# A decoder layer with 32 experts: gate and up weights in f16 halves, their bound by a matmul, the splits spread over an expert's two blocks

## The chip, the core and the metric

The kernel runs on one core of a Trainium2 chip. The metric is the device time of one execution in microseconds (us); lower is better. Engines are named as in the profile: PE (TensorE matmul) with PEld (its weight loads), DVE (VectorE), ACT (ScalarE), POOL (GpSimd) and SP (SyncE), which here only issues DMAs.

## What is computed

One hybrid decoder layer on 4096 tokens of width 1024, in float32 from outside. First a mixer (attention with a window of 128, and a gated short convolution), then a mixture of 32 experts: a router picks one group of four and two of its eight experts, so that there are 8192 pairs of a token and an expert. They are sorted by expert and worked off in blocks of 128 rows, each of one expert:

```
def expert_block(args):
    xb, e = args
    return (jax.nn.silu(xb @ w_g[e]) * (xb @ w_u[e])) @ w_d[e]

ybuf = lax.map(expert_block, (xbuf.reshape(n_blocks, MOE_BLK, D_MODEL), block_e))
y = ybuf.reshape(n_blocks * MOE_BLK, D_MODEL)[dest] * gate_s[:, None].astype(xt.dtype)
return jax.ops.segment_sum(y, tok_s, num_segments=n_tok)
```

`w_g` and `w_u` are 1024 x 512 for each expert and `w_d` is 512 x 1024, 2 MB each. The change touches this second half, the expert stage, alone.

## The kernel before, in words

**Precision.** A product of two float32 matrices is made of three matmuls: each operand is split into a high part (the value rounded to a narrower type) and a low part (what is left), and hi x hi, hi x lo and lo x hi are added up in PSUM. In the mixer (helper at L574) both parts are f16, and the operands are scaled by powers of two so that f16 can hold them. In the expert stage (helper `split_mm`, matmuls at L1676) both parts are fp32r, a float32 with a shortened mantissa, and nothing needs scaling. The profile shows an fp32r matmul as f32.

**One block of 128 rows on PE** (`tensor`, `block_`): 24 matmuls into psA (rows x gate weights), 4 transposes into psE of the previous block's product (`turn_act`, L1691), 24 matmuls into psB (rows x up weights), 8 transposes into psC and psD of the next block's rows (`transpose_rows`, L1684), and 24 matmuls into psF and psG (`down`), which are the down product of the block before. All matmuls have 512 columns. The first block of an expert follows the last of the expert before without a pause in the program.

**Splitting the weights.** SP loads an expert's three weights as float32 into `wi_all` (one buffer for each; `load_expert`, L172). ACT makes the high part (`split`, L1770, eight pieces of 512 columns, with a conversion to fp32r), DVE the low part as raw minus high (L1812, eight pieces). All of it is in the expert's first block: gate before that block's matmuls, up behind it, down at the end, when the down product of the expert before is done. There is one set of high and low parts for each weight, so the split of an expert's gate waits until the last psA of the expert before has been computed (`gate_ps`). SP issues the next load as soon as the split has read the buffer.

**The rest of a block.** On ACT and DVE, in their program order: `copy_y` (the down result of two blocks back, scaled by the row's gate, ACT L1777 and DVE L1819), `turn` (the transposed product in high and low part, L1789 and L1830), `silu` on ACT (L1783) and `product` on DVE (L1826), `turn_x` (the transposed rows in two parts, L1796 and L1836).

**The chain of the rows, on POOL** (`gpsimd`, `block_`): `shift` moves three short columns of indices along (two copies, L1617 and L1620); a DMA fetches the block's 128 slot entries (L1632); when they have landed and the transposes of the block before have read `xg`, an indirect DMA gathers the block's rows (`xg<-hn_rows`, L1600, 512 KB); when `copy_y` is done, POOL copies the row numbers (L1609) and an indirect DMA adds `y` to the output (L1612, 512 KB); then POOL waits until the gathered rows have landed and turns to the next block. PE's `transpose_rows` waits for those rows. Everything on POOL is in this one order.

**How many blocks.** `blocks_of` holds each expert's number of blocks, at least 1 (2 for expert 0). Every engine reads it and loops (`walk`).

**Passing from the mixer to the experts.** Each engine waits in `mixed` for the last table entries. Expert 0's three loads are issued before that. POOL then fetches the first slot entries and the first rows, and PE can begin.

## Time and profile before

| | us |
|---|---|
| median of 3 runs | 2751.67 (2751.11 to 2752.50) |
| the profiled execution, own time | 2750.93 |
| its span, first to last instruction | 2749.3 |
| PE busy in the span | 2643.6 (96%) |
| DVE busy | 1716.2 (62%) |
| ACT busy | 1391.3 (51%) |
| POOL busy | 798.8 (29%) |
| granted TensorE clock, mean of the span | 0.987 |

The profiled execution took 1.6 us more than its span, and lies 0.7 us under the median. A matmul's length in the profile reaches to its modelled end, and successive matmuls overlap; what one costs PE is the distance of the starts. In rows of the timeline with a count (x24), the piece's length reaches from the first start to the last end. In the chain of waits the pieces follow on each other, so that there a row's length is the time it takes of the span.

### The profile page before, as it was taken

Reading aid. Unit: us, or ns where it says so; the run is one execution under the profiler, and the core shown is the slowest. Engines: PE = TensorE matmul, PEld = TensorE weight load, DVE = VectorE, ACT = ScalarE, POOL = GpSimd, SP = SyncE. Lnnn points to the kernel's source line nnn. Section 1 sums busy time; section 2 is a strip of 40 time slices with the busy share of each in tenths; the row PEclk is TensorE's granted clock in tenths of the full one; section 3 lists DMA queues with packets and bytes.
Section 4 is the critical chain, followed back from the end, with each engine's and each line's share of the span. In section 5 each row is a group of like instructions: output and inputs, shape, how many; then the busy total and the mean of one; then the engine's idle time right before and its main releaser. Section 6 shows DMA issues by size and latency. Waiting matters only on the chain.

```text
span 2749.3 us, 49924 instructions
## 1 busy us (share of the span) xinstructions
PE 2643.6 (96%) x14252; PEld 1820.9 (66%) x14253; DVE 1716.2 (62%) x3920; ACT 1391.3 (51%) x3046; POOL 798.8 (29%) x825
## 2 busy tenths in 40 slices
PE   4999999999999999996699999999999999999997
PEld 2455555555555555553588888888888888888886
DVE  5677777777777777776454455545655444546633
ACT  7666555565555566553344445445545333435533
POOL 1122323232322222331232333323223323333232
PEclk9999999999999999998799999999999999999999
DMA  8376555556655555656556677667767665667763
GB/s 315 82 166 166 156 160 158 152 157 165 163 152 160 154 156 164 166 138 167 187 169 189 186 236 244 200 196 224 235 186 232 205 183 153 194 180 237 235 181 54
DMA packets 546395, 495.22 MB, mean 180 GB/s; under 512 B 411787, under 2 KB 411948, under 8 KB 545340
## 3 DMA queue, kind: packets, MB, share of 16 engines
q1 hardware_dynamic: 517516, 406.08, 49.2%
q0 software_dynamic: 28848, 88.77, 13.8%
q8 instruction: 14, 0.23, 0.0%
q14 instruction: 17, 0.14, 0.0%
HBM read 309.74 MB, written 87.88 MB: 145 GB/s over the span
## 4 chain that ended last, share of the span: by engine, by line
PE 89%; DVE 3%; DMA 3%; ACT 2%; issue 1%; SPq 1%; POOL 1%; POOLq 0%; DVEq 0%; ACTq 0%
PE psB L1676 15%; PE psA L1676 15%; PE psG L574 11%; PE psF L1676 7%; PE psG L1676 7%; PE psE L574 6%; PE psF L574 6%; PE psD L574 6%; PE psC L574 6%; PE psH L574 3%; PE psC L1684 1%; PE psD L1684 1%; PE psE L1691 1%; DMA xg<-hn_rows,slots 1%; DMA slots<-slot_table 1%
## 5 line engine op out<-in xcount | busy, mean ns | idle before, releaser
L574 PE MATMUL psG<-wi_all,both_xT 128*128 128x512 f16 x1536 | 345.2, 382 | 10.9 <-DMA both_xT<-x 10.9
L574 PEld LDWEIGHTS psG<-wi_all,both_xT 128*128 128x128 f16 x1536 | 148.7, 98 | 188.2 <-DMA both_xT<-x 11.1
L1600 POOL DMA_INDIRECT xg<-hn_rows,slots x80 | 99.2, 1240 | 544.0 <-DMA slots<-slot_table 389.4
L1676 PE MATMUL psB<-up_hi,gT_hi 128*128 128x512 f32 x632 | 254.4, 402 | 0.0
L1676 PE MATMUL psA<-gate_hi,gT_hi 128*128 128x512 f32 x632 | 247.3, 391 | 3.1 <-ACT gT_hi L1796 1.7
L1812 DVE TENSOR_TENSOR down_lo<-wi_all,down_hi 128x512 fp32r<-128x512 f32 x256 | 157.0, 686 | 147.1 <-ACT down_hi L1770 147.1
L1676 PE MATMUL psB<-up_hi,gT_lo 128*128 128x512 f32 x632 | 247.6, 392 | 0.0
L1676 PE MATMUL psA<-gate_hi,gT_lo 128*128 128x512 f32 x632 | 247.3, 391 | 0.0
L1676 PE MATMUL psA<-gate_lo,gT_hi 128*128 128x512 f32 x632 | 247.0, 391 | 0.0
L1676 PE MATMUL psB<-up_lo,gT_hi 128*128 128x512 f32 x632 | 246.4, 390 | 0.0
L1796 ACT ACTIVATE gT_hi<-psC 128x512 fp32r<-128x512 f32 x80 | 47.8, 597 | 384.8 <-PE psC L1684 384.8
L1826 DVE TENSOR_TENSOR act_rows<-psB,gated 128x512 f32<-128x512 f32 x79 | 54.6, 691 | 289.6 <-PE psB L1676 289.6
L1770 ACT ACTIVATE down_hi<-wi_all 128x512 fp32r<-128x512 f32 x256 | 137.0, 618 | 149.1 <-PE psG L1676 149.1
L819 ACT ACTIVATE prob<-prob,soft,s_stat 128x256 f32<-128x256 f32 x256 | 150.6, 589 | 94.2 <-DVE soft L1206 94.1
L1609 POOL COPY rows_of_y<-slots 128x1 int32<-128x1 int32 x80 | 129.3, 1616 | 236.9 <-DVE y L1819 236.2
L1812 DVE TENSOR_TENSOR gate_lo<-wi_all,gate_hi 128x512 fp32r<-128x512 f32 x256 | 157.0, 686 | 46.2 <-ACT gate_hi L1770 46.2
L574 PE MATMUL psE<-wo_all,both_mT 128*128 128x512 f16 x768 | 178.5, 383 | 5.9 <-DMA both_mT<-prob 5.9
L574 PE MATMUL psC<-wi_all,both_xT 128*128 128x512 f16 x792 | 178.6, 381 | 4.5 <-DVE wi_all L1186 4.5
L574 PE MATMUL psD<-wi_all,both_xT 128*128 128x512 f16 x792 | 178.2, 380 | 0.0
L574 PE MATMUL psF<-wo_all,both_mT 128*128 128x512 f16 x768 | 176.2, 379 | 0.0
L1770 ACT ACTIVATE gate_hi<-wi_all 128x512 fp32r<-128x512 f32 x256 | 137.0, 618 | 44.5 <-issue 44.5
L1812 DVE TENSOR_TENSOR up_lo<-wi_all,up_hi 128x512 fp32r<-128x512 f32 x256 | 156.7, 685 | 1.0 <-ACT up_hi L1770 1.0
(320 smaller groups left out, 5777.2 us busy)
## 6 DMA issues: line engine op xcount, KB each, us to landing
wi_all<-in_w_gate SPq DMA_DIRECT2D x32, 2048.0 KB, 9.5
wi_all<-in_w_up SPq DMA_DIRECT2D x32, 2048.0 KB, 12.9
wi_all<-in_w_down SPq DMA_DIRECT2D x32, 2048.0 KB, 11.7
xt<-in_x SPq DMA_DIRECT2D x32, 512.0 KB, 3.7
um<-u_rows SPq DMA_DIRECT2D x64, 256.0 KB, 2.7
out_rows<-h SPq DMA_DIRECT2D x32, 512.0 KB, 3.0
xres<-in_x SPq DMA_DIRECT2D x31, 512.0 KB, 4.1
hn_rows<-xres SPq DMA_DIRECT2D x31, 512.0 KB, 2.9
```

Source lines behind the costliest of these rows:

```text
L574: m = nc.tensor.matmul(ps, left[:, l, k, :], weights.half(r, k, n, width), start=(k == opens and j == 0), stop=(k == closes and j == 2))
L819: s.activation(prob[:, hd, :], prob[:, hd, :], ACT.Exp, bias=ntop[:, hd:hd + 1], scale=inv_s, accum_out=psum_[:, hd:hd + 1]).then_inc(p_sb ...
L1600: pool.indirect_dma_start(xg[:], None, hn_dram, bass.IndirectOffsetOnAxis(ap=slots[:, 0, 0:1], axis=0), bounds_check=SEQ + P - 1).then_inc ...
L1609: g.tensor_copy(rows_of_y[:], slots[:, 3, 0:1]).then_inc(named, 1)
L1676: m = nc.tensor.matmul(ps[:, :], l[:, k, :], r[:, r_k[n], :], start=(n == 0 and j == 0), stop=(n == len(l_k) - 1 and j == 2))
L1684: m = nc.tensor.transpose(ps[:, c * P:(c + 1) * P], xg[:, (4 * h + c) * P:(4 * h + c + 1) * P], ident)
L1691: m = nc.tensor.transpose(psE[:, c * P:(c + 1) * P], act_rows[:, c * P:(c + 1) * P], ident)
L1770: s.activation(hi[n][:, k, :], raw[n][:, k, :], ACT.Copy).then_inc(hi_s[n], 1)
L1796: s.activation(gT_hi[:, 4 * h:4 * h + 4, :].rearrange("p k c -> p (k c)"), ps[:, :], ACT.Copy).then_inc(xgT_hi, 1)
L1812: v.tensor_tensor(lo[n][:, k, :], raw[n][:, k, :], hi[n][:, k, :].bitcast(F32), ALU.subtract).then_inc(lo_s[n], 1)
L1826: v.tensor_tensor(act_rows[:], psB[:, :], gated[:], ALU.mult).then_inc(act_s, 1)
```

## The change

Gate and up are now in f16 parts. Since f16 has a small range, each of the two is multiplied by a power of two before the split, and the result is divided by it (`scale=inverse` in `silu`, and in `product`); the rows are scaled in `turn_x` by the known `hn_scale`. The power of two comes from a bound of the weights: ACT sums the absolute values of each partition's 4096 weights (`sum_up`, with a bf16 result that nobody reads), and the largest of the 128 sums is needed on every partition. For expert 0 POOL finds it (`partition_all_reduce`). For the others DVE masks the sums down to powers of two and spreads them on a diagonal (`spread_bound`), PE multiplies a matrix of ones with it (`every_bound`, 256 columns into psH), and DVE takes the maximum of the row and makes scale and inverse in five dependent steps (`scales`).

Gate and up have two raw buffers and two sets of parts (`p`), and are prepared an expert ahead: in the first block of expert e the gate of e+1 is split, in its second block the up of e+1; sums are taken another expert ahead. `down` stays in fp32r with one buffer, split in the first block. All splits are now two pieces of 2048 columns. Every expert has at least two blocks. PE waits for a whole weight, not for pieces of it.

The core of the diff; further hunks carry the scale into `silu`, `product` and `turn_x`, and unroll `walk` over pairs of experts:

```diff
-        step(v.tensor_scalar(blocks_of[:, counts], blocks_of[:, E:], 1, None, ALU.max))
-        step(v.tensor_scalar(blocks_of[:, 0:1], blocks_of[:, 0:1], 2, None, ALU.max))
+        step(v.tensor_scalar(blocks_of[:, counts], blocks_of[:, E:], 2, None, ALU.max))
...
-    hi = {n: sb(f"{n}_hi", [P, 8, 512], F32R) for n in raw}
-    lo = {n: sb(f"{n}_lo", [P, 8, 512], F32R) for n in raw}
+    hi = {n: [sb(f"{n}_hi_{p}", [P, 8, 512], F16) for p in range(2)] for n in SCALED}
+    lo = {n: [sb(f"{n}_lo_{p}", [P, 8, 512], F16) for p in range(2)] for n in SCALED}
+    hi["down"], lo["down"] = ([sb(f"down_{w}", [P, 8, 512], F32R)] * 2 for w in ("hi", "lo"))
...
+        def next_loads(e, p):
+            reload("gate", e + 1, 1 - p, 2)
+            reload("down", e, 0, 1)
+            reload("up", e + 1, 1 - p, 2)
+
+        sp.wait_ge(summed, 2)
+        for n in SCALED:
+            load_expert(sp, n, 1, 1)
         mixed(sp)
...
+        pool.wait_ge(summed, 2)
+        pool.partition_all_reduce(most(0), sums(0), P, RMAX).then_inc(most_s, 1)
         mixed(pool)
...
+        def every_bound(e):
+            pe.wait_ge(diagonal_s, 2 * e)
+            nc.tensor.matmul(every_row, ones[:, :], diagonal[:, :], start=True, stop=True).then_inc(every_s, 1)
...
+            if follow and (second if is_zero(e) else first):
+                every_bound(e + 1)
             if not static0:
                 turn_act(b)
...
+            s.activation(junk, raw[n][p].rearrange("p k n -> p (k n)"), ACT.Abs, accum_out=sums(p, n)).then_inc(summed, 1)
...
+            for c in range(CHUNKS):
+                s.activation(chunk(hi[n][p], c), chunk(raw[n][p], c), ACT.Copy, scale=power(p, n)).then_inc(hi_s[n], 1)
...
+            if is_zero(e) and first:
+                turn_x(b + 1)
+                sum_up("gate", 1, 1, 0, junk)
+                sum_up("up", 1, 1, 0, junk)
+                split_down(e, b)
...
+            v.tensor_scalar(most(p).bitcast(I32), sums(p).bitcast(I32), 0x7F800000, None, ALU.bitwise_and).then_inc(masked, 1)
+            dve.wait_ge(masked, e)
+            for c in range(2):
+                v.tensor_scalar(diagonal[:, c * P:(c + 1) * P], ident, most(p)[:, c:c + 1], None, ALU.mult).then_inc(diagonal_s, 1)
...
+                v.scalar_tensor_tensor(chunk(lo[n][p], c), chunk(raw[n][p], c), power(p, n), chunk(hi[n][p], c),
+                                       ALU.mult, ALU.subtract).then_inc(lo_s[n], 1)
```

How the order moves on the engines. On ACT, in an expert's first block before: gate split (L1770), `copy_y` (L1777), up split, `turn` (L1789), `silu` (L1783).

```order
343 L1768 ISA [waits gate_ps]
344 L1770 ACTIVATE gate_hi<-wi_all 128x512 [waits raw_in_gate]
345 L1770 ACTIVATE gate_hi<-wi_all 128x512 x7
346 L1774 ISA
347 L1775 REGISTER_ALU [waits y_ps]
348 L1776 ISA [waits shifted]
349 L1777 ACTIVATE y<-psF,slots 128x512 [waits added]
350 L1770 ACTIVATE up_hi<-wi_all 128x512 [waits raw_in_up,up_ps]
351 L1770 ACTIVATE up_hi<-wi_all 128x512 x7
352 L1788 REGISTER_ALU [waits aT_ps]
353 L1789 ACTIVATE aT_hi<-psE 128x512 [waits y_ps]
```

The same place now, from `silu` on: the gate split of the next expert (L1809), the rows (L1842), a sum (L1803, its junk result in `up_hi`), and the down split (L1816).

```order
360 L1829 ACTIVATE gated<-psA,own 128x512 [waits act_s,gate_ps]
361 L1807 ISA
362 L1809 ACTIVATE gate_hi<-wi_all,own 128x2048 [waits step_s]
363 L1809 ACTIVATE gate_hi<-wi_all,own 128x2048
364 L1841 ISA [waits up_ps]
365 L1842 ACTIVATE gT_hi<-psC,rt_stat 128x512 [waits xgT_ps]
366 L1841 REGISTER_ALU
367 L1842 ACTIVATE gT_hi<-psD,rt_stat 128x512 [waits xgT_ps]
368 L1800 ISA
369 L1802 REGISTER_ALU [waits raw_in_gate_1]
370 L1803 ACTIVATE up_hi,own<-wi_all 128x4096 [waits summed]
```

The up split has left this block for the second one, and no split stands ahead of `copy_y` any more. On DVE, at expert 0's first two blocks now: product, rows, the down split in two pieces (L1947), the mask (L1931) and the diagonal (L1935), and then the maximum over PE's answer (L1920).

```order
L1962 SCALAR_TENSOR_TENSOR act_rows<-psB,own,gated 128x512 [waits up_ps,silu_s]
L1973 SCALAR_TENSOR_TENSOR gT_lo<-psC,rt_stat,gT_hi 128x512 [waits xgT_hi]
L1973 SCALAR_TENSOR_TENSOR gT_lo<-psD,rt_stat,gT_hi 128x512 [waits xgT_hi]
L1947 TENSOR_TENSOR down_lo<-wi_all,down_hi 128x2048 [waits hi_s_down] x2
L1931 TENSOR_SCALAR own<-own 128x2 [waits summed]
L1935 TENSOR_SCALAR diagonal<-cst,own 128x128 [waits masked]
L1935 TENSOR_SCALAR diagonal<-cst,own 128x128
L1920 TENSOR_REDUCE own<-psH 128x2 [waits every_s]
```

PE's matmul for the bound waits for the diagonal, and so for all that stands above it here; PE does nothing else meanwhile, since it too is in program order.

## Rows read from the trace of the kernel before

**Rows 1.** The page: PE's busy time; costliest groups: ScalarE's silu, one a block.

```profile
PE 2643.6 (96%) x14252; PEld 1820.9 (66%) x14253; DVE 1716.2 (62%) x3920; ACT 1391.3 (51%) x3046; POOL 798.8 (29%) x825
...
L1783 ACT ACTIVATE gated<-psA 128x512 f32<-128x512 f32 x79 | 46.8, 593 | 4.0 <-PE psA L1676 4.0
```

**Rows 2.** Chain that ended last, two late blocks: start us, us, what.

```profile
2692.97 5.44 PE psA L1676 x24
2698.42 0.44 PE psE L1691 x4
2698.86 5.49 PE psB L1676 x24
...
2710.68 5.44 PE psA L1676 x24
```

**Rows 3.** Timeline of PE in the mixer: start us, us, instructions.

```profile
409.53 5.34 PE L574 MATMUL psG<-wi_all,both_xT 128*128 128x512 f16 x24
414.71 2.78 PE L574 MATMUL psH<-wi_all,both_xT 128*128 128x256 f16 x24
```

**Rows 4.** Timeline of ACT: gate splits of an expert of two blocks and its successor.

```profile
1856.32 4.28 ACT L1770 ACTIVATE gate_hi<-wi_all 128x512 fp32r<-128x512 f32 x8 [1.13 <-issue]
...
1891.78 4.28 ACT L1770 ACTIVATE gate_hi<-wi_all 128x512 fp32r<-128x512 f32 x8 [1.18 <-issue]
```

**Rows 5.** Groups by line: ACT and DVE work on other widths.

```profile
L791 ACT ACTIVATE wi_all<-wi_all 128x2304 bf16<-128x2304 f32 x8 | 17.0, 2122 | 4.7 <-DMA wi_all<-in_w_in 4.7
L779 ACT ACTIVATE x<-xt,stat 128x1024 f16<-128x1024 f32 x33 | 37.9, 1148 | 1.1
L1276 DVE SCALAR_TENSOR_TENSOR x<-xt,stat,x 128x1024 f16<-128x1024 f32 x33 | 42.2, 1280 | 8.5 <-ACT x L779 8.5
L1327 DVE SCALAR_TENSOR_TENSOR q<-qsq,q 128x512 f16<-128x512 f32 x32 | 22.2, 693 | 5.9 <-ACT q L891 5.4
```

**Rows 6.** Timeline around an expert's second block (psA from 1877.5): DVE, SP, POOL, PE.

```profile
1883.28 0.75 DVE L1819 TENSOR_SCALAR y<-psG,slots 128x512 f32<-128x512 f32 x1
1883.51 0.37 SPq L172 DMA_DIRECT2D wi_all<-in_w_down  x1
1885.49 1.65 POOL L1612 DMA_INDIRECT out_rows<-y,rows_of_y  x1 [0.96 <-DMA xg<-hn_rows,slots]
1888.53 0.59 POOL L1632 DMA_DIRECT2D slots<-slot_table  x1 [0.85 <-POOL slots L1620]
1896.84 1.89 POOL L1600 DMA_INDIRECT xg<-hn_rows,slots  x1 [7.71 <-DMA slots<-slot_table]
1898.36 4.90 DVE L1812 TENSOR_TENSOR up_lo<-wi_all,up_hi 128x512 fp32r<-128x512 f32 x8
1898.76 4.55 POOL L1609 COPY rows_of_y<-slots 128x1 int32<-128x1 int32 x1
...
1906.58 0.60 PE L1684 MATMUL psC<-cst,xg 128*128 128x128 f32 x4
```

**Rows 7.** By tile, from issue to landing: the 80 gathers (xg); then y's.

```profile
DMA to landing us min/median/max: 4.2/4.5/9.8
...
DMA to landing us min/median/max: 5.9/9.9/11.1
```

**Rows 8.** Timeline at the start of the experts: POOL and SP.

```profile
1318.77 0.62 POOL L1632 DMA_DIRECT2D slots<-slot_table  x1 [5.41 <-DVE y L1844]
1321.69 1.21 POOL L1600 DMA_INDIRECT xg<-hn_rows,slots  x1 [2.30 <-DMA slots<-slot_table]
1322.79 0.38 SPq L172 DMA_DIRECT2D wi_all<-in_w_gate  x1
...
1333.65 1.09 POOL L1600 DMA_INDIRECT xg<-hn_rows,slots  x1 [5.39 <-DMA slots<-slot_table]
```

**Rows 9.** Timeline of PE: after an idle time, and just behind.

```profile
1275.64 5.04 PE L574 MATMUL psE<-wo_all,both_mT 128*128 128x512 f16 x12 [5.86 <-DMA both_mT<-prob]
1280.52 2.75 PE L574 MATMUL psF<-wo_all,both_mT 128*128 128x512 f16 x12
```

More of the change, by code:

```diff
@@ new lines, in is_zero, with split_up, reload @@
+    def is_zero(e):
+        return isinstance(e, int) and e == 0
+    def sync(sp):
+        def split_up(n, e):
+            sp.wait_ge(hi_s[n], CHUNKS * (e + 1))
+            sp.wait_ge(lo_s[n], CHUNKS * (e + 1))
+        def reload(n, e, p, ahead):
+            split_up(n, e)
+            load_expert(sp, n, e + ahead, p)
+        def next_loads(e, p):
[5 more added lines that the diff above has]
+            load_expert(sp, n, 1, 1)
+        mixed(sp)
+        reload("gate", 0, 0, 2)
+        reload("up", 0, 0, 2)
+        with sp.Fori(0, (E - 4) // 2) as pair:
+            next_loads(pair * 2, 0)
+            next_loads(pair * 2 + 1, 1)
+        next_loads(E - 4, 0)
+        reload("down", E - 3, 0, 1)
+        reload("down", E - 2, 0, 1)
@@ L1782, in silu @@
                 act.wait_ge(act_s, b)
-            s.activation(gated[:], psA[:, :], ACT.Silu).then_inc(silu_s, 1)
+            s.activation(gated[:], psA[:, :], ACT.Silu, scale=inverse(p, "gate")).then_inc(silu_s, 1)
         def turn(b):
@@ L1796, in turn_x, with block_ @@
                 s.activation(gT_hi[:, 4 * h:4 * h + 4, :].rearrange("p k c -> p (k c)"), ps[:, :],
-                             ACT.Copy).then_inc(xgT_hi, 1)
+                             ACT.Copy, scale=hn_scale).then_inc(xgT_hi, 1)
+        def block_(e, i, b, p, r, follow):
+            known = isinstance(b, int)
+            first, second = isinstance(i, int) and i == 0, isinstance(i, int) and i == 1
+            junk = hi["up"][1 - p][:].rearrange("p k n -> p (k n)").bitcast(BF16)
+            if not (known and b < 2):
+                copy_y(b)
+            if not (known and b == 0):
+                turn(b)
+            silu(b, p)
+            if is_zero(e) and first:
[3 more added lines that the diff above has]
+                split_down(e, b)
+            elif is_zero(e) and second:
+                split("gate", 1, 1)
+                turn_x(b + 1)
+                sum_up("gate", 2, 0, 1, junk)
+                sum_up("up", 2, 0, 1, junk)
+                act.wait_ge(summed, 6)
+                split("up", 1, 1)
+            elif first:
+                if follow:
+                    split("gate", e + 1, 1 - p)
+                turn_x(b + 1)
+                if follow > 1:
+                    sum_up("gate", e + 2, p, r + 1, junk)
+                split_down(e, b)
+            elif second:
+                if follow > 1:
+                    sum_up("up", e + 2, p, r + 1, junk)
+                turn_x(b + 1)
+                if follow > 1:
+                    act.wait_ge(summed, 2 * (e + 3))
+                if follow:
+                    split("up", e + 1, 1 - p)
+            else:
+                turn_x(b + 1)
@@ L1799, in scalar @@
         s.preload_act_table_set("silu_and_others")
+        for c, n in enumerate(SCALED):
+            sum_up(n, 0, 0, 0, wi_flat[:, 12288 + c * 2048:12288 + (c + 1) * 2048].bitcast(BF16))
         mixed(act)
         act.sem_inc(y_act, 3)
-        halves(act, split, copy_y, silu, turn, turn_x)
+        split("gate", 0, 0)
+        turn_x(0)
+        split("up", 0, 0)
+        total = walk(act, block_)
+        copy_y(total)
+        turn(total)
+        copy_y(total + 1)
     def vector(dve):
@@ L1835, in turn_x, with block_ @@
                 dve.wait_ge(xgT_hi, 2 * b + h + 1)
-                v.tensor_tensor(gT_lo[:, 4 * h:4 * h + 4, :].rearrange("p k c -> p (k c)"), ps[:, :],
-                                gT_hi[:, 4 * h:4 * h + 4, :].rearrange("p k c -> p (k c)").bitcast(F32),
-                                ALU.subtract).then_inc(xgT_lo, 1)
+                hold(dve, held)
+                v.scalar_tensor_tensor(gT_lo[:, 4 * h:4 * h + 4, :].rearrange("p k c -> p (k c)"), ps[:, :], hn_scale,
+                                       gT_hi[:, 4 * h:4 * h + 4, :].rearrange("p k c -> p (k c)"),
+                                       ALU.mult, ALU.subtract).then_inc(xgT_lo, 1)
+        def block_(e, i, b, p, r, follow):
+            known = isinstance(b, int)
+            first, second = isinstance(i, int) and i == 0, isinstance(i, int) and i == 1
+            if not (known and b < 2):
+                copy_y(b)
+            if follow and (second if is_zero(e) else first):
+                scales(e + 1, 1 - p)
+            if not (known and b == 0):
+                turn(b)
+            if follow and (second if is_zero(e) else first):
+                split("gate", e + 1, 1 - p)
+            product(b, p)
+            turn_x(b + 1)
+            if first:
+                split_down(e)
+            if is_zero(e) and first:
+                spread_bound(1, 1)
+            if second and follow:
+                split("up", e + 1, 1 - p)
+            if second and follow > 1:
+                spread_bound(e + 2, p)
         v.memset(slots[:], 0).then_inc(cleared, 1)
@@ L1842, in vector @@
         v.tensor_copy(slots[:, :, 0], cst[:, C_JUNK:C_JUNK + 1].to_broadcast([P, 4])).then_inc(cleared, 1)
+        scales(0, 0)
         mixed(dve)
+        v.memset(ones[:], 1.0)
         v.memset(y[:], 0.0).then_inc(cleared, 1)
         dve.sem_inc(y_dve, 3)
-        halves(dve, split, copy_y, product, turn, turn_x)
+        split("gate", 0, 0)
+        turn_x(0)
+        split("up", 0, 0)
+        total = walk(dve, block_)
+        copy_y(total)
+        turn(total)
+        copy_y(total + 1)
     return dict(sync=sync, tensor=tensor, scalar=scalar, gpsimd=gpsimd, vector=vector)
```

220 lines of the change are left out of this document (124 added, 96 removed).

## The prediction

> **What bounds the kernel now.** I read the page first: PE is busy for 96% of the span [rows 1], so only what shortens or interrupts PE counts. Then the chain of waits, for one late block [rows 2]: from one psA (2692.97) to the next (2710.68) are 17.71 us, in which every piece follows on the last with no gap. There are 79 blocks, with one silu each [rows 1]; 78 x 17.71 = 1381 of the 2749 us. Inside, 24 matmuls of psA take 5.44 us, 0.227 us each, and the 24 of psB 5.49. The mixer has the other price: 24 f16 matmuls of the same 512 columns run from 409.53 to 414.71, 5.18 us or 0.216 each [rows 3]. ACT and DVE are half idle over the span, but the splits come in bursts, and POOL's chain of the rows has little room in it: these decide whether PE gets its gain.
>
> **The change, part by part.**
>
> *Cheaper matmuls.* In each block 48 of 72 matmuls become f16. Gain (5.44 - 5.18) x 2 = 0.52 us a block, x 79 = 41 us. The first psB matmul stands behind short transposes, so that its weight load shows: psB takes 0.05 more than psA [rows 2]. An f16 load is quicker; I take 0.07 us a block, 6 us (bounds 0 and 12). Together -47.
>
> *More blocks?* Not here. The 32 gate splits in the trace of ACT never start closer than 35 us, which is two blocks, and 1856.32 to 1891.78 [rows 4] is such a pair. The new minimum of two adds none.
>
> *The bound on PE.* 31 matmuls of 256 columns. In the mixer 24 such columns-of-256 go from 414.71 to 417.33, 0.109 each. With a weight load that may show behind it 0.14, x 31 = +4 (bounds 3 and 7).
>
> *ACT and DVE in the steady state.* Prices: ACT takes 1148 ns for 1024 columns to f16 with a scale, and 2122 for 2304 to bf16 [rows 5]. Between them 2048 columns come to 2.0 us, and a sum over 4096, at the same 0.8 to 0.9 ns a column, to 3.8 with its read-out. DVE takes 693 and 1280 ns [rows 5]: 2.4 to 2.5 us for 2048. Now walk through an expert of two blocks, F being the start of its first psA. PE: psA ends at 5.2, bound 5.3, psB ends 11.0, transposes 11.9, down 17.3. DVE: scales in five steps 5.5 to 6.9. ACT: `turn` and `silu` to 7.0, gate split to 11.0, rows 11.5 to 12.6, gate sum to 16.4, down split from 17.4 to 21.2. DVE: `turn` to 7.6, low gate 9.1 to 13.9, product 14.6, rows 15.9. The next psA needs those rows at 17.3: room 1.4. Second block, T = 17.3: DVE ends the low down at T+6.8 and `copy_y` at T+7.4; the down product needs them at T+11.7. ACT: up sum T+6.9 to T+10.7, rows to T+12.5, up split to T+16.4. DVE: low up to T+19.3, 2.2 into the next expert; PE needs it at T+22.7. The diagonal follows 1 us later, needed at T+22.3. So nothing stops PE: 0, and the cover is these rooms of 1.4 to 4 us. One expert's splits and sums are 19 us of ACT in 34.4, beside 6 of small work.
>
> *POOL's chain.* `copy_y` of the second block ends at T+7.4. Before, from its end (1884.03) to the issue of the slot entries (1888.53) are 4.5 us, and 7.7 + 0.6 later (1896.84) the gather starts [rows 6]. So slot entries at T+11.9, gather at T+20. Its rows are needed at the next block's transposes, T+17.1+11.0 = T+28.1: the gather may take 8. The median is 4.5, the longest 9.8 [rows 7]. The gather of [rows 6] is one of the long: issued at 1896.84, it feeds transposes that start at 1906.58, just in time. Behind it POOL's copy stands for 4.55 us, until DVE's run of low parts ends (1903.3). I read both as POOL being held up by DVE. In the changed order DVE's low up ends at T+19.3, ahead of this gather, and the next copy waits for a `copy_y` with no split near. What is new is the up load, issued at T+19.4, just ahead of the gather. y's adds to the output, the size of a gather, show what a load does: 5.9 at best, 9.9 in the median [rows 7], and the one of [rows 6] goes out 2 us behind a load. With two thirds of that surcharge I take 7.5 for the gather: the rows land at T+27.5, and in some of the 28 experts that have an up load there PE waits a little. +4 (bounds 0 and 28 x 1.7 = 48, for 9.8).
>
> The Trainium skill, "GPSIMD Engine Reference", section Specifications, has the SBUF interfaces of POOL shared with DVE, in contention when a DVE instruction has two SBUF inputs. By that rule each low part of 2.4 us can hold up a POOL copy falling into it; the 4.55 us of [rows 6] agree. If the rule caught the copies of every second block, PE would lose what the second rival below has; by the walk it doesn't.
>
> *The start, gather.* Before, the first slot entries are issued at 1318.77 and the gather starts at 1321.69 [rows 8], with no load in flight. Now POOL waits for two sums on ACT (7.7 us together, begun when the mixer lets go of ACT some 10 us ahead of those slot entries, so to about 1317) and the reduction, of which I assume 0.5: slot entries at about 1319.5. And SP issues two loads, 4 MB, at 1317. The next gather shows what that does: POOL waited 5.39 us for its slot entries, issued some 5 us after the load of 1322.79, against 2.30 for the first [rows 8]. With two loads ahead I take 8 us to landing. First rows at about 1334.5 instead of 1326.4: +8 (bounds +3 and +14).
>
> The skill speaks for less. "DMA: Bandwidth & Descriptors", section Queues, rings and completion order, says that each DMA engine takes turns between queues packet by packet, so that a small transfer would wait for one packet of a load and not for the load. By that rule the start would lose some 3 us, and the sum would be 5 lower. The 5.39 of [rows 8] lies nearer to a whole load, so I keep 8.
>
> *The start, bound.* The stall this change adds in plain sight. S is the psA start of expert 0's second block. ACT ends the rows at S-1, takes two sums (7.7) and the two pieces of the down split (3.8); DVE's second low piece ends at S+13.2, the diagonal at S+14.1. PE stands at S+5.2, waiting for that diagonal, with the transposes and psB queued behind it. +8.9. After 5.86 us without work PE took 5.04 us for 12 matmuls that take 2.75 right after [rows 9]: it had come back at the lower of its clocks, 1.2 GHz. The same here: +2.3. Together +11.
>
> *Sum.* 2750.9 - 47 + 4 + 4 + 8 + 11 = 2731, for an execution 0.7 us under the median of the runs, which I leave uncorrected. Tail and mixer stay.
>
> **The rivals.**
>
> 1. *The rows come late in every expert* (slower). Place: PE's transposes in an expert's first block, when their gather starts just behind an up load. Price: as it takes 9.8 instead of 7.5, T+29.8 against T+28.1, 1.7 x 28 = 48, less the 4 counted: 2731 + 44 = 2775. It decides from about 8.6 us on, where the loss is 0.5 an expert and more; above 9.2 the kernel is slower. For it: the longest gathers, and the adds' median. Against: the long gathers seem to have another cause, DVE, which the new order takes away. 0.13.
>
> 2. *DVE's splits run longer* (no change). A low part could cost as much as the slowest work of its kind in the trace, 1.66 ns a column, 3.4 us. Then the low gate ends at F+15.9, the rows at F+17.9, and PE stands 0.6 in 31 experts, 19 us: 2750. Against: that happens beside POOL's long products in the mixer, which the expert stage hasn't. With halves of rival 1, 0.13.
>
> 3. *The start is hidden.* The slot entries pass the loads, and the diagonal is ready earlier than I count: 2731 - 16 = 2715. Against: both are in program order. 0.08.
>
> 4. *f16 gives nothing here*, because something else than the operand's type sets 0.227: 2731 + 41 = 2772. The mixer's even 5.18 speaks against. 0.02.
>
> **How the numbers follow.** My forecast, 0.64: 2731, with 2722 to 2743 from its own bounds (gather 4 at the start, small waits 0 to 10). The range has to leave out no more than 0.2: downwards it takes in most of rival 3, upwards rival 2 and the lighter half of rival 1, 2718 to 2758. A change of 0.2%, 5.5 us, is what a measurement of this kernel can tell from none. Faster by more: forecast and rival 3, 0.72. Within: rival 2, 0.13. Slower: rivals 1 and 4, 0.15.
>
> **What the profile after would show.** A late block of 17.1 us in the chain, psA and psB at 5.18 to 5.2 (else rival 4). PE idle once for about 9 us at L1761, in the second block of the stage, released by DVE's diagonal, with the granted clock at half behind it. The first gather's rows at about 1334. PE's idle time for `xg` under 10 us in total; if it is 30 or more, with gathers of 9 us, rival 1. If PE waits for DVE's gT_lo in first blocks, and the low parts take over 3 us, rival 2. By the sum the expert stage, from its first psA to its last psG, is 28 us shorter than before; if it is not 15 to 40 shorter, the sum is wrong.

## The result, and the profile after

The changed kernel takes 2793.5 us (median of 4 runs, 2790.9 to 2800.0), the one before 2751.6 beside it: ratio 1.0155, 95% interval 1.0136 to 1.0175. It is slower by 42 us, where 2731 was predicted and 2758 was the end of the range. The profiled execution took 2790.9, its span 2789.3.

The page, engine times, chain by engine, and the group of POOL's gathers (total us, mean ns, idle before):

```profile
PE 2625.4 (94%) x14283; PEld 1494.0 (54%) x14284; DVE 1759.5 (63%) x3598; ACT 1603.3 (57%) x2598; POOL 738.2 (26%) x826
...
PE 72%; DMA 13%; DVE 5%; ACT 3%; issue 3%; POOL 1%; SPq 1%; POOLq 1%; ACTq 0%; DVEq 0%
...
L1651 POOL DMA_INDIRECT xg<-hn_rows,slots x80 | 129.3, 1616 | 446.9 <-DMA slots<-slot_table 216.2
```

PE is busy 18 us less than in [rows 1] (38 less in the run without low parts, e2_reduce, where it stalls only at the start: matmuls at the lower clock count as busy for longer), and its share is lower all the same: it waits. The groups by line say for what (PE's transposes of the rows and the bound's matmul) and give the prices of the new pieces:

```profile
L1733 PE MATMUL psC<-cst,xg 128*128 128x128 f32 x320 | 52.7, 291 | 67.0 <-DMA xg<-hn_rows,slots 66.5
...
L1761 PE MATMUL psH<-diagonal,ones 128*128 128x256 bf16 x31 | 8.6, 276 | 8.1 <-DVE diagonal L1935 8.1
...
L1803 ACT ACTIVATE up_hi<-wi_all 128x4096 bf16<-128x4096 f32 x62 | 224.2, 3617 | 0.2
L1941 DVE SCALAR_TENSOR_TENSOR up_lo<-wi_all,own,up_hi 128x2048 f16<-128x2048 f32 x64 | 147.7, 2349 | 42.1 <-ACT up_hi L1809 42.1
L1809 ACT ACTIVATE gate_hi<-wi_all,own 128x2048 f16<-128x2048 f32 x64 | 124.7, 1995 | 15.0 <-DVE own L1924 15.0
```

Of the 66.5 us for rows, 23.6 are the one wait at the start; 42.8 are ten waits of 4.0 to 4.4 us and one of 0.2 in the steady part.

The sharpest measure is the distance from one silu (ScalarE, once a block) to the next, 78 of them. Before they sum to 1379.2 us, 17.68 each. After, 66 of them are 16.2 to 17.7, mean 17.21; **two at the start are 23.2 and 20.8; and ten more are 23.0 to 24.3.** Against 17.1 each the ten cost 63.4 us and the two 9.8. So 1379.2 - 38.2 + 63.4 + 9.8 = 1414.2, and the first psA begins 6.8 us later (1336.63 against 1329.82): +41.8. The way from the first psA to the first silu is 1.4 us shorter than before, the tail 0.4: 40.0, which is the difference of the two spans.

Nine of the ten fall into the second block after an expert of two blocks, behind three gathers in a row of 8 us or more. The tenth, the earliest, falls into the second block after expert 0, where the rows come after slots entries of 6.0 and 6.5 us and a gather of 10.0. Not every expert of two blocks brings one: of sixteen (the last expert left out) seven bring none, and each of these directly follows one that did, whose stall has moved the next gathers off the loads. The chain of waits through one of the ten (start us, us, what):

```profile
1911.10 5.20 PE psA L1725 x24
1916.30 0.44 PE psE L1740 x4
1916.73 5.18 PE psB L1725 x24
...
1927.95 1.72 DVE up_lo L1941
1929.67 9.29 DMA xg<-hn_rows,slots
...
1940.77 1.57 POOL slots_old L1668
...
1943.47 6.11 DMA slots<-slot_table
...
1950.57 9.98 DMA xg<-hn_rows,slots
1960.55 0.04 issue
1960.60 1.11 PE psC L1733 x4
1961.71 0.85 PE psD L1733 x4
1962.57 3.49 PE psF L1725 x12
1966.05 2.72 PE psG L1725 x12
```

psA and psB cost 5.20 and 5.18, as forecast. Then two gathers of 9.3 and 10.0 us, with a slots entry of 6.1 and a copy of 1.6 between them, are one serial chain on POOL, from 1929.67 to 1960.55. From the start of one gather to the start of the next are 20.9 us, where a block leaves 17.1. PE waits 4.2 us for the second, and comes back at the lower clock. Stretches behind it (us, busy, then granted clock, DMA share, GB/s):

```profile
1958.00:1960.00 2.00, 0.00 (x0) 0.00 (x0) 0.00 (x0) 0.00 (x0) 0.00 (x0) 1.00 0.94 301
1960.00:1962.00 2.00, 1.40 (x7) 1.40 (x8) 0.00 (x0) 0.25 (x1) 0.37 (x2) 0.65 1.07 281
1962.00:1964.00 2.00, 2.00 (x7) 1.68 (x6) 1.32 (x2) 1.83 (x3) 0.59 (x1) 0.50 0.79 171
1964.00:1966.00 2.00, 2.00 (x10) 1.60 (x9) 0.86 (x2) 2.00 (x2) 0.76 (x1) 0.99 0.00 0
```

A granted clock of 0.50 is 1.2 GHz; the transposes and psF take 5.45 us there, and some 3.65 in a block without a stall.

What meets the gathers: SP's queue in the same stretch, all loads of 2 MB.

```profile
1908.07 0.37 SPq L172 DMA_DIRECT2D wi_all<-in_w_gate  x1
...
1930.44 0.37 SPq L172 DMA_DIRECT2D wi_all<-in_w_up  x1
1942.53 0.37 SPq L172 DMA_DIRECT2D wi_all<-in_w_gate  x1
1952.27 0.37 SPq L172 DMA_DIRECT2D wi_all<-in_w_down  x1
```

The gathers start at 1906.55, 1929.67 and 1950.57. **Each of three gathers in a row has a load issued 1.5, 0.8 and 1.7 us behind it**, and they land after 9.9, 9.3 and 10.0 us. Of 80 gathers 47 take 8 us or more; before, 9 did.

### The profile page after: what moved, and what is told of

It is laid out like the page before. It is cut to its first block, busy times and chain, and to the rows that moved or that the text cites. A ratio compares the mean times of both kernels' runs of the same rounds, so it can differ in the third digit from the quotient of the medians.

```text
span 2789.3 us, 48388 instructions
## 1 busy us (share of the span) xinstructions
PE 2625.4 (94%) x14283; PEld 1494.0 (54%) x14284; DVE 1759.5 (63%) x3598; ACT 1603.3 (57%) x2598; POOL 738.2 (26%) x826
## 4 chain that ended last, share of the span: by engine, by line
PE 72%; DMA 13%; DVE 5%; ACT 3%; issue 3%; POOL 1%; SPq 1%; POOLq 1%; ACTq 0%; DVEq 0%
PE psG L575 11%; PE psB L1725 9%; PE psA L1725 9%; DMA xg<-hn_rows,slots 8%; PE psE L575 6%; PE psF L575 6%; PE psD L575 6%; PE psC L575 6%; PE psF L1725 5%; PE psG L1725 5%; DMA slots<-slot_table 4%; PE psH L575 3%; DVE up_lo L1941 1%; PE psC L1733 1%; PE psD L1733 1%
## 5 line engine op out<-in xcount | busy, mean ns | idle before, releaser
L575 PE MATMUL psG<-wi_all,both_xT 128*128 128x512 f16 x1536 | 345.2, 381 | 11.2 <-DMA both_xT<-x 11.2
L1725 PE MATMUL psA<-gate_hi,gT_hi 128*128 128x512 f16 x632 | 241.0, 381 | 3.7 <-issue 2.0
L1725 PE MATMUL psB<-up_hi,gT_hi 128*128 128x512 f16 x632 | 240.5, 381 | 0.0
L1725 PE MATMUL psB<-up_lo,gT_hi 128*128 128x512 f16 x632 | 240.3, 380 | 0.0
L1725 PE MATMUL psB<-up_hi,gT_lo 128*128 128x512 f16 x632 | 240.3, 380 | 0.0
L1725 PE MATMUL psA<-gate_lo,gT_hi 128*128 128x512 f16 x632 | 240.0, 380 | 0.0
L1725 PE MATMUL psA<-gate_hi,gT_lo 128*128 128x512 f16 x632 | 240.0, 380 | 0.0
L1803 ACT ACTIVATE up_hi<-wi_all 128x4096 bf16<-128x4096 f32 x62 | 224.2, 3617 | 0.2
L1947 DVE TENSOR_TENSOR down_lo<-wi_all,down_hi 128x2048 fp32r<-128x2048 f32 x64 | 143.8, 2288 | 109.3 <-ACT down_hi L1816 109.3
L1941 DVE SCALAR_TENSOR_TENSOR up_lo<-wi_all,own,up_hi 128x2048 f16<-128x2048 f32 x64 | 147.7, 2349 | 42.1 <-ACT up_hi L1809 42.1
L1941 DVE SCALAR_TENSOR_TENSOR gate_lo<-wi_all,own,gate_hi 128x2048 f16<-128x2048 f32 x64 | 147.7, 2349 | 42.1 <-ACT gate_hi L1809 42.1
L1842 ACT ACTIVATE gT_hi<-psC,rt_stat 128x512 f16<-128x512 f32 x80 | 55.0, 687 | 171.5 <-PE psC L1733 170.6
```

The source lines that it names most:

```text
L575: m = nc.tensor.matmul(ps, left[:, l, k, :], weights.half(r, k, n, width), start=(k == opens and j == 0), stop=(k == closes and j == 2))
L1725: m = nc.tensor.matmul(ps[:, :], l[:, k, :], r[:, r_k[n], :], start=(n == 0 and j == 0), stop=(n == len(l_k) - 1 and j == 2))
L1803: s.activation(junk, raw[n][p].rearrange("p k n -> p (k n)"), ACT.Abs, accum_out=sums(p, n)).then_inc(summed, 1)
L1842: s.activation(gT_hi[:, 4 * h:4 * h + 4, :].rearrange("p k c -> p (k c)"), ps[:, :], ACT.Copy, scale=hn_scale).then_inc(xgT_hi, 1)
L1941: v.scalar_tensor_tensor(chunk(lo[n][p], c), chunk(raw[n][p], c), power(p, n), chunk(hi[n][p], c), ALU.mult, ALU.subtract).then_inc(lo_s[n ...
L1947: v.tensor_tensor(chunk(lo["down"][0], c), chunk(raw["down"][0], c), chunk(hi["down"][0], c).bitcast(F32), ALU.subtract).then_inc(lo_s["do ...
```

## The experiments

Theory T1: the load in flight makes the gathers long, and PE late. Rival T2: DVE's long two-input low parts hold POOL, whatever the loads do. A joint theory, that it takes both, came out of the first runs. "Sum" is that of the 78 silu distances; "held" counts gathers whose issue on POOL lasts 1.5 us or more instead of 1.06. Sum and counts are those of one profiled execution.

| kernel | us | sum | gathers over 8 us | held | distances over 20 us |
|---|---|---|---|---|---|
| before | 2751.6 | 1379.2 | 9 | 12 | 0 |
| after | 2793.5 | 1414.2 | 47 | 37 | 12 |
| e1_gated | 2739.6 | 1357.6 | 1 | 29 | 3 |
| e2_reduce | 2733.8 | 1351.1 | 9 | 2 | 2 |
| e3_start | 2790.1 | 1416.8 | 49 | 40 | 12 |
| e4_later | 2791.4 | 1408.7 | 49 | 37 | 10 |
| e5_f16 | 2719.8 | 1345.1 | 13 | 16 | 0 |
| e6_all | 2728.0 | 1354.9 | 1 | 29 | 1 |
| e7_spread | 2793.4 | 1414.2 | 45 | 39 | 12 |
| e8_best | 2726.4 | 1353.4 | 1 | 28 | 2 |
| e9_f16_held | 2723.5 | 1352.7 | 2 | 11 | 2 |
| e10_pieces | 2730.1 | 1354.4 | 31 | 31 | 3 |
| e11_ahead | 2736.1 | 1350.9 | 30 | 23 | 2 |
| e12_f16_ahead | 2715.8 | 1342.6 | 16 | 4 | 1 |

Runs are medians of 4; before, beside them, 2752.3 to 2755.0.

### e1_gated: loads held back

```diff
-            reload("gate", e + 1, 1 - p, 2)
+            reload("gate", e + 1, 1 - p, 2, first_in)
             reload("down", e, 0, 1)
-            reload("up", e + 1, 1 - p, 2)
+            reload("up", e + 1, 1 - p, 2, second_in)
```

SP waits besides until the rows of expert e+1's first, or second, block have landed, which POOL counts in two new semaphores.

> The changed kernel, but SP issues an expert's gate load only when the rows of the next expert's first block have landed, and its up load when those of the next expert's second block have; the down load comes behind the gate load in the same queue. Theory T1 (the late rows in ten experts come from the gather of rows, 512 KB, being in flight together with a 2 MB expert load that is issued within about 2 us of it: 8.4 to 10.4 us instead of 4.5, twice in a row in experts of two blocks): the gathers take 4.4 to 5.5 us, the ten silu gaps of 23 to 24.3 us outside the first expert go back to 17.1 to 17.6, the time falls by about 62 us to some 2730. Rival T2 (DVE's long two-input low parts hold POOL's gather descriptors and copies, whatever the loads do): gathers stay at 8 us or more, ten long gaps stay, time 2785 to 2795. If the loads now arrive too late for ACT's sums, new stalls show on ACT and the time is between.

Measured: 2739.6 us, ratio to before 0.9939 (0.9922 to 0.9956). DVE's work is untouched and 29 gathers are still held at issue, but they now take 4.9 to 6.5 us (one, at the start, 10.2), and no long distance is left behind the fourth. POOL's gather in the place that corresponds to 1950.57:

```profile
1930.80 2.22 POOL L1654 DMA_INDIRECT xg<-hn_rows,slots  x1 [4.46 <-DMA slots<-slot_table]
1935.26 0.19 POOL L1663 COPY rows_of_y<-slots 128x1 int32<-128x1 int32 x1 [2.24 <-DVE y L1959]
```

T2 alone falls. DVE's low part of down starts at 1929.80 in two pieces of 2.29: the gather is held to the end of the first, 1932.09, and 0.94 us beyond. The time missed 2730 by 10: the first four distances (24.5, 20.9, 16.6, 21.7) are 6.4 us more than the changed kernel's, and in this execution the mixer ended 6 us later.

### e2_reduce: DVE's low parts with one input

```diff
+                if not isinstance(e, int):
+                    v.tensor_reduce(scrap[:, c:c + 1], chunk(raw[n][p], c), AX, ALU.max).then_inc(lo_s[n], 1)
+                    continue
```

> The changed kernel, but from expert 2 on DVE's low parts of gate and up (two-input, 2.35 us each) are left out: in their place stands a maximum over the same 2048 raw elements into a scratch column, with the same semaphores, so the low matmuls read the low parts of the first experts. T1 (gather and load collide): gathers with a load issued within 2 us still take 8.4 to 10 us, though their issue on POOL falls to 1.06 us; at least seven of the ten long gaps stay; time 2765 to 2793. T2 (DVE holds POOL): gathers back to 4.5 us, no long gap, time about 2730.

The kernel leaves these low parts out; the maximum in their place keeps DVE busy for 2.28 us instead of 2.35.

Measured: 2733.8, 0.9923 (0.9907 to 0.9940). T1 alone falls too. The loads come as before, but the gathers' issue is down to 1.06 us, and a load issued 1.4 us behind them hurts no more: they take 4.2 to 4.8 us, where the changed kernel has 9.2 to 10.0 with a load 1.5 us behind. With the load 0.1 to 0.8 us behind they still take 4.8 to 8.8. So it is both: **the load has to fall into the gather's issue, and DVE's low part stretches that issue until it does.** Gathers of the 14 profiles, by when the next load is issued (count, median, lowest to highest, us):

| load behind the gather's start by | issue under 1.5 us | issue 1.5 us or more |
|---|---|---|
| no load from 9 ahead to 5 behind | 372: 4.4 (4.2 to 7.5) | 100: 5.3 (4.7 to 6.5) |
| 0 to 0.9 | 99: 8.9 (4.8 to 10.1) | 32: 9.2 (8.4 to 9.7) |
| 0.9 to 1.6 | 28: 4.5 (4.2 to 7.1) | 116: 9.7 (8.3 to 10.2) |
| 1.6 to 1.9 | 9: 4.8 (4.6 to 7.7) | 19: 10.0 (9.8 to 10.5) |

The DMA packets in the traces say what decides: whose packets start first. POOL's transfers are in queue q0, SP's loads in q1. First the changed kernel from the start of the gather at 1906.55 to 1911.95, then the kernel without low parts from the start of such a gather, at 1881.79 (issue 1.06 us, load 1.4 behind), until it has landed, at 1886.25 (packets, MB, share of the 16 engines):

```profile
q1 hardware_dynamic: 343, 0.70, 46.9%
...
q0 software_dynamic: 144, 0.52, 39.8%
q1 hardware_dynamic: 78, 0.16, 15.5%
```

In the first, 343 packets of the load have started before the first of the gather, which comes at 1911.97; in the second the gather's 144 go ahead. A gather's first packet comes 0.70 us after the end of its issue when nothing is in the way, a load's most often 1.0 to 1.2 us after its own issue. **Of 282 gathers with a load issued up to 2.6 us behind their start, no other load issued in the 11 us before and no add of `y` in flight (all profiles but e9_f16_held, the first three gathers left out), 222 had it issued 0.37 us or more before the end of their own issue, and took 5.8 to 11.2 us; the 60 others had it 0.24 before that end at the earliest, and took 4.2 to 5.3.** The load overtakes, and a held issue gives it the time to.

The two are bound to meet: SP issues a load when DVE's low part ends, and a gather that falls into a piece of it is held to that piece's end. In the changed kernel, a gate's low part and the gather:

```profile
1903.21 4.61 DVE L1941 SCALAR_TENSOR_TENSOR gate_lo<-wi_all,own,gate_hi 128x2048 f16<-128x2048 f32 x2 [1.34 <-ACT gate_hi L1809]
...
1906.55 2.21 POOL L1651 DMA_INDIRECT xg<-hn_rows,slots  x1 [6.69 <-PE psD L1733]
```

DVE ends at 1907.82, the load follows at 1908.07, and POOL's issue ends at 1908.76. The Trainium skill, "SBUF — State Buffer", section "SBUF: two separate sides", has such starvation for transfers whose descriptors GpSimd writes while DVE holds the port pair they share; the 2.21 against 1.06 us agree. The Trainium skill, "DMA: Bandwidth & Descriptors", section "Queues, rings and completion order", has the DMA engines take turns between queues; by that rule alone a load 0.5 us behind would be no worse than one 1.4 behind, and the rows differ, 8.9 against 4.5. Between 1909.09 and 1911.97 no turn of the gather is seen; whether its packets were ready by then the trace doesn't tell.

### e3_start: late first loads

```diff
         sp.wait_ge(summed, 2)
+        mixed(sp)
+        sp.wait_ge(rows_in, 16)
         for n in SCALED:
             load_expert(sp, n, 1, 1)
-        mixed(sp)
```

> The changed kernel, but the early loads of expert 1's gate and up are issued only when the first rows have landed. The first slots entry takes 2 to 3 us instead of 5.1, the first gather 4.5 instead of 5.6; the first psA begins 3 to 6 us sooner against the mixer's end. By T1 the rest of the run is unchanged or one long gap more or less: 2784 to 2790. If the start was not held by these loads (T2 has no loads in it): within 2 us of 2791.

Measured: 2790.1, 1.0130 (1.0113 to 1.0147). From the mixer's last psH to the first psA are 23.1 us instead of 27.5 (before 21.7), so the loads did cost 4.4. The first distance grew to 24.4 and gave 1.2 of it back.

### e4_later: the bound of expert 1 later

PE's `every_bound(1)` goes behind `transpose_rows`, DVE's `scales` and both gate splits behind `turn_x`, in expert 0's second block only.

> The changed kernel, but in expert 0's second block the bound's matmul stands behind PE's transposes of the next rows, and the scales and the gate split behind the turn of x on DVE and ACT. If the 8.1 us wait of PE for the diagonals, with the half clock behind it, cost the 9.8 us that the two first silu gaps are over 17.1 each: the first two gaps together fall from 44.0 to 34 to 37 us and the time falls by 7 to 10 us, to 2781 to 2784. If that block waits for its rows anyway (T1: the gathers of that stretch are long too), under 3 us.

Measured: 2791.4, 1.0133 (1.0111 to 1.0155): no gain. The wait moved on; PE's long waits now (its idle time in brackets):

```profile
1369.23 0.28 PE L1761 MATMUL psH<-diagonal,ones 128*128 128x256 bf16 x1 [1.59 <-DVE diagonal L1937]
...
1393.74 0.77 PE L1725 MATMUL psF<-down_hi,aT_hi 128*128 128x512 f32 x1 [6.20 <-DVE aT_lo L1968]
```

DVE, with scales and the gate split now at the end of that block, comes 6.2 us late to the next block's `turn`.

### e5_f16: f16 halves alone

```diff
-    hi = {n: sb(f"{n}_hi", [P, 8, 512], F32R) for n in raw}
+    hi = {n: sb(f"{n}_hi", [P, 8, 512], F32R if n == "down" else F16) for n in raw}
```

The same for `lo` and for `gT_hi`, `gT_lo`, in the kernel before; no scaling.

> The kernel before, with one thing changed: the halves of gate, up and of the turned rows are f16 instead of f32r, without scaling; sums, bounds, the spread splits and the earlier loads are all left out. Step of the prediction: psA and psB of 24 matmuls take 5.2 us instead of 5.45 each, so 41 to 47 us less: 2704 to 2710, if the loads and gathers stay where they were. T1: a shorter block shifts the loads against the gathers a little, but DVE and ACT keep the short pieces of 512, and the second block's gather keeps its room; at most one or two long gaps. T2: same. If the f16 gain itself is missing (the rival that f16 gives nothing): 2750.

Measured: 2719.8, 0.9880 (0.9863 to 0.9896). A late block of its chain:

```profile
2611.46 5.20 PE psA L1676 x24
2616.66 0.44 PE psE L1691 x4
2617.10 5.18 PE psB L1676 x24
...
2628.65 5.20 PE psA L1676 x24
```

17.19 us instead of 17.71 [rows 2], x 78 = 41. It gains 32.5; some 7 us go into distances of 17.4 to 18.1. Thirteen gathers take 8 us or more, each with a gate load issued between 0.4 us ahead of its start and 1.3 behind. They are what the 2704 to 2710 expected left out.

### e6_all: e1_gated, e3_start and e4_later together

> The changed kernel with the three edits together: loads held until rows have landed, first loads after the first rows, the bound of expert 1 behind the transposes. T1 and the prediction's terms for start and bound: 2791 less 62, less 3 to 6, less 7 to 10, so 2712 to 2720. T2: above 2765.

Measured: 2728.0, 0.9910 (0.9893 to 0.9926), outside the 2712 to 2720 expected; of the 59 us by which the sum falls, to 1354.9, the held loads alone give 57. In the first blocks PE waits 6.24 us for `aT_lo`, as in the run with the bound later.

### e7_spread: the diagonals before down's low parts

`spread_bound(1, 1)` stands ahead of `split_down(0)` on DVE.

> The changed kernel, but in expert 0's first block DVE makes the diagonals of expert 1 before the low parts of down, not behind them. If PE's wait of 8.1 us for the diagonal comes from DVE's order (4.5 us of low parts and ACT's down halves ahead of it), that wait falls to 0 to 3 us, the first silu gap from 23.2 to 17 to 19 us, and no later gap grows by as much: time 2782 to 2786. If ACT's second sum (the up weights landing late) is what sets it, the wait stays over 5 us and the time within 3 us of 2791.

Measured: 2793.4, 1.0144 (1.0127 to 1.0161), where 2782 to 2786 was expected. PE's wait for the diagonal is gone, the first distance falls only to 21.1, the second grows to 21.5, and the time is the same. In its place:

```profile
1351.96 0.66 PE L1733 MATMUL psC<-cst,xg 128*128 128x128 f32 x4 [2.54 <-DMA xg<-hn_rows,slots]
1355.06 0.58 PE L1725 MATMUL psA<-gate_hi,gT_hi 128*128 128x512 f16 x1 [2.01 <-issue]
```

The second rows came late, and some twelve matmuls behind them ran at the lower clock.

### e8_best: e1_gated, e3_start and e7_spread together

> The changed kernel with three edits: loads held until rows have landed, expert 1's first loads after the first rows, and the diagonals before down's low parts. Expected from the runs with the loads held and with the late first loads: 2740 less 4 for the start, less 6 to 9 for the two first blocks: 2724 to 2730; if the late first loads set the second sum now, 2730 to 2736.

Measured: 2726.4, 0.9903 (0.9886 to 0.9919). The first four distances together are 7 to 15 us over 17.1 each in every one of these versions, whatever is moved there.

### e9_f16_held: f16 alone, gate load held

```diff
                 sp.wait_ge(lo_s[n], 8 * e)
+                if n == "gate":
+                    sp.wait_ge(second_in, 8 * e)
```

POOL counts `second_in` up when the rows of an expert's second block have landed. This kernel and e12_f16_ahead also ask for two blocks of every expert, which each has anyway.

> The kernel before with f16 halves alone (as in the run of that kind, 2720), and besides its gate load held until the rows of the same expert's second block have landed. There 13 gathers still took 8 us or more, each with a gate load issued 0 to 0.8 us behind it while DVE made up's low parts, and the silu gaps over 17.2 us summed to about 7 us. By the joint theory (load right behind a gather, and DVE's low part stretching the gather's issue) no gather is over 7 us and the time is 2712 to 2716. If those gaps come from POOL's copies under DVE's work instead, the gathers shorten but the gaps stay: 2718 to 2722.

Measured: 2723.5, 0.9890 (0.9863 to 0.9916): a miss. The holding SP queue lets gate and up loads go together, half a microsecond apart, and the slots entry then stands behind 4 MB. POOL there:

```profile
1865.33 0.60 POOL L1636 DMA_DIRECT2D slots<-slot_table  x1 [0.77 <-POOL slots L1624]
1874.38 1.12 POOL L1604 DMA_INDIRECT xg<-hn_rows,slots  x1 [8.45 <-DMA slots<-slot_table]
```

8.45 us for 1 KB, and its gather took 7.1.

### e10_pieces: eight short pieces instead of two long

`CHUNKS = 8` instead of 2.

> The changed kernel with all halves made in eight pieces of 512 elements instead of two of 2048. Joint theory (what counts is that DVE is at a two-input low part while POOL issues the gather, and that the load follows on its end): pieces back to back hold POOL as two long ones do, the gather's issue still takes over 1.5 us in some 30 blocks, eight or more long gaps stay, time 2785 to 2800. Rival T3 (only one long instruction holds POOL, short ones let it in between): issue 1.06 to 1.3 us, gathers of 4.5 to 5 us with the load 1.4 us behind, at most three long gaps, 2735 to 2750.

Measured: 2730.1, 0.9911 (0.9894 to 0.9927): 63 us won by one constant. The joint theory's number fell, and T3's range is missed by 5 us on the better side, though only half of its reason holds. The gather that meets the gate's low part goes free:

```profile
1870.82 5.39 DVE L1941 SCALAR_TENSOR_TENSOR gate_lo<-wi_all,own,gate_hi 128x512 f16<-128x512 f32 x8
...
1875.41 1.07 POOL L1651 DMA_INDIRECT xg<-hn_rows,slots  x1 [4.83 <-PE psD L1733]
```

0.80 us of DVE's run are left at its start, and it is issued in 1.07 us; in the changed kernel, with one long piece, a gather with 0.8 us left took 1.79. What counts is the piece that runs when the gather starts, here with 0.14 us left. Where more than 0.12 us of a piece are left, the issue ends 0.94 us after the end of that piece in 322 of 322 cases with long pieces and in 131 of 169 with short ones (all profiles, the first three gathers left out). The load comes 1.0 us behind, and the gather lands in 4.5 us instead of 9.9. With down's pieces too a gather got in early (3.6 us of the run left, issue 1.53; with long pieces 2.34). But the one that meets the up's low part is held through one piece more, the last, to 1898.80 and 0.94 us beyond, and takes 9.6:

```profile
1893.42 5.38 DVE L1941 SCALAR_TENSOR_TENSOR up_lo<-wi_all,own,up_hi 128x512 f16<-128x512 f32 x8
...
1897.69 2.06 POOL L1651 DMA_INDIRECT xg<-hn_rows,slots  x1 [6.42 <-DMA slots<-slot_table]
```

31 gathers still take 8 us or more. That the time is down nonetheless is the point: the first of the three bad gathers in a row takes 5 us less, so the third starts earlier beside down's low part, its load comes 3.8 us behind it instead of 1.7, and it takes 4.9. Only the one in the middle stays long, and the ten stalls are one (22.5). In that one the second and the third are long, 8.7 and 10.2, so two in a row can be enough.

### e11_ahead: the slots entry one block ahead

```diff
-            pool.dma_start(slots[:, 0, :], table[bass.ds(e * CAP + i * P, P), :]).then_inc(slots_in, 16)
+            if fixed and not (known and b == 0):
+                pool.wait_ge(slots_in, 16 * (b + 1))
...
+                g.tensor_copy(slots[:, 0, :], ahead[:, i, :]).then_inc(placed, 1)
...
             gather()
+            if fixed and i == 0:
+                pool.dma_start(ahead[:, 1, :], table[bass.ds(e * CAP + P, P), :]).then_inc(slots_in, 16)
...
```

Behind the gather of a second block POOL fetches the entry of the next expert's first block in the same way.

> The changed kernel, loads and splits untouched, but POOL fetches the slots entry of an expert's first and second block one block ahead (a copy of 0.2 us takes the place of the fetch of 2 to 7 us between the landing of one block's rows and the next gather). If a gather of 9 to 10 us only hurts because that fetch stands in series with it on POOL (entry 6.2, gather 10, copies 1.6 to 4 us: more than the 17.1 us of a block), then gathers of 8 us or more stay, as many as in the changed kernel or more, but the ten long silu gaps vanish: 2726 to 2733. If the long gather alone makes the rows late, the gaps stay: 2780 to 2793.

Measured: 2736.1, 0.9938 (0.9921 to 0.9954), 3 us over the 2726 to 2733 expected. 30 gathers still take 8 us or more, and not one costs anything: behind the third no distance is over 17.4. A bad one, and who releases it now:

```profile
1914.62 0.19 POOL L1689 COPY slots<-ahead 128x2 int32<-128x2 int32 x1 [0.33 <-POOL slots L1673]
1918.02 2.22 POOL L1653 DMA_INDIRECT xg<-hn_rows,slots  x1 [3.22 <-PE psD L1749]
```

The gather goes out as soon as PE has read the last rows. The sum equals that of the run without low parts; the median is 2 us over it, and in this execution a load 1.8 us behind the very first gather made it 10.5 us.

### e12_f16_ahead: the same on e5_f16

> The kernel before with f16 halves alone (2720) and the slots entry fetched one block ahead in the same way. Its silu gaps of 17.4 to 18.1 us, 7 us in sum over 17.2, come from gathers that are issued late behind the entry's fetch and then meet the gate load. Expected: no gap over 17.3 us outside the first blocks, 2711 to 2715. If the gaps come from POOL's copies that wait through DVE's low parts, they stay: 2718 to 2722.

Measured: 2715.8 (2709.0 to 2719.3), 0.9856 (0.9839 to 0.9872), the fastest kernel of the study; with the f16 halves alone it was 0.9880 (0.9863 to 0.9896), so the intervals overlap and that it beats that one isn't shown. It misses the 2711 to 2715 expected by 1 us, and one distance of 22.5 is left in its profile, at a third block, whose entry isn't fetched ahead.

## Why the prediction was wrong

**Failed: POOL's chain.** The prediction walked one gather, that of the up load, and priced it at 7.5 us, +4. The chain cost 63. Three things were wrong with it.

- *Its price and its cause.* "I read both as POOL being held up by DVE" and "In the changed order DVE's low up ends at T+19.3, ahead of this gather". The low part ends at 1930.3, T+19.2, as walked, but the gather starts at 1929.67, 0.6 us before that and not at T+20. It took 9.3 us. The hold alone makes 4.7 to 6.5.
- *The ones not walked.* Gate and down loads follow on DVE's low parts just as the up load does, and the gathers they met, one ahead of the up's and one behind it, took 9.9 and 10.0 us.
- *The stall's place.* The 9.3 us gather landed at T+28, just in time, as the walk would have had it. The next one was late: entry 6.1, copy 1.6, gather 10.0 in series. The added slots entry of [rows 6] was in the walk once, not as a term that recurs.

The trace of before had the other half of the cause. Its gather of 1896.84 [rows 6] took 9.6 us with a gate load issued 1.2 us behind it, a row that the reading left out:

```profile
1898.01 0.37 SPq L172 DMA_DIRECT2D wi_all<-in_w_gate  x1
```

All nine of its gathers of 8 us or more have a gate load 0.5 to 1.4 us behind their start; the six others whose issue took 1.5 us or more landed in 4.7 to 4.9, with the next load 2.1 or more behind.

Rival 1, "the rows come late in every expert", had the right resource, and 0.13 of the chance. It had the wrong count, 28 for ten: experts of three blocks recover, with a gather that meets no load, and of the experts of two blocks in a row every other one is spared. And its price lacked the clock: ten stalls at 6.3 us, of which some 4 are the wait (4.2 in the chain above) and 2 the lower clock behind it. Measured +63 where the sum had +4.

**Right, by the prediction's own steps.** psA and psB at 5.20 and 5.18. Blocks without a stall are 17.21 in the mean, the bound's matmul included, against 17.68. That makes -38 over the 78 distances, where -47 and +4, so -43, were taken. The further 6 us for psB's first weight load are not there: a late block of f16 alone is 17.19, against the 17.12 of the working. No more blocks. The sum 3.8 us and the halves 2.0 on ACT, as taken; DVE's 2.35 a little under it, so rival 2 is out. Start: +6.8 for +8, of which 1.0 is that the mixer ended later in this execution (slots entry 5.1, where 8 was taken; gather 5.6). Bound: an idle 8.1 us for 8.9, 9.8 with the clock for 11. But moving that wait away gave nothing in two runs, since DVE's `turn` or the second rows are late next; the term was its own size by luck of what lies behind it.

**The signs to look for** were the right ones: PE's idle time for `xg` "30 or more, with gathers of 9 us" is what the page shows. The expert stage was to be 28 us shorter, and is 33 longer (1439.9 from first psA to the end of the last psG, before 1406.6).

**What stays open.** That the load's packets get in ahead is shown; why the gather's then start only 1.8 to 4.3 us after its issue has ended, and not in turn with the load's, is not. Why a gather beside the up's short pieces is held through one more piece and one beside the gate's isn't known either. Why the first blocks stay over 17.1 with the diagonal out of the way was followed in one execution only.

## What to carry to other kernels

When a change makes a load's trigger and a small indirect transfer's trigger follow on the same event, look at the order of the two within a microsecond, and walk every such pair, not the one in view. When a transfer is long in the trace of before, list what every queue issued within 2 us of it before naming a cause. A serial chain on POOL (entry, gather, copies) is safe only if its worst links together fit the block; fetching the index one block ahead made 30 long gathers free, for a copy of 0.2 us. And try the cheap half of a change alone: f16 operands in the old order gave 0.988, the full change 1.0155.

## What was not expected of the hardware

- A gather of 512 KB takes 4.4 us, 5.3 held by DVE, 8.9 with a 2 MB load issued under 0.9 us behind its start, 4.5 with the load 0.9 to 1.6 us behind, and 9.7 if it is held as well. What divides them is whether the load is issued 0.37 us or more before the gather's issue ends (222 cases, 5.8 to 11.2 us) or 0.24 before it and later (60 cases, 4.2 to 5.3).
- A two-input DVE instruction holds a gather's issue to its own end and 0.94 us beyond: 2.2 us with 1.3 left of a long piece, 1.06 without. Where more than 0.12 us of a piece were left, POOL got in behind that piece in 322 of 322 cases with long pieces and 131 of 169 with short ones. A one-input maximum over the same data holds nothing, 1.06.
- One constant, two pieces or eight, moved the kernel by 63 us, by way of two gathers in three.
- A slots entry of 1 KB takes 3.0 us in the median with no load near (2.0 at the least), 6.1 (5.3 to 7.1) with one issued up to 2 us before it, 8.1 (5.1 to 9.6) with two issued up to 4 us before.
